# An expert stage without engine barriers: the overfill flag loaded ahead, routing constants first, softmax weights behind the selection

## The reference

```python
def moe_swiglu(h, w_router, w_gu_e, w_dn_e):
    logits = (h @ w_router).astype(jnp.float32)          # 256 x 8
    top_val, top_idx = lax.top_k(logits, TOP_K)          # 2 of 8
    top_w = jax.nn.softmax(top_val, axis=-1)
    combine = jnp.sum(jax.nn.one_hot(top_idx, N_EXPERTS) * top_w[..., None], axis=-2)
    out = jnp.zeros_like(h)
    for e in range(N_EXPERTS):
        out = out + combine[..., e:e + 1] * swiglu(h, w_gu_e[e], w_dn_e[e])
    return out
```

## Time and profile before

| | us |
|---|---|
| median of 3 runs | 2953.33 |
| lowest, highest | 2951.13, 2954.88 |
| profiled execution, its own time | 2958.39 |
| its span in the trace | 2956.6 |
| PE busy, share of the span | 2781.0, 94% |
| DVE, ACT, POOL busy | 1777.8, 1478.7, 39.9 |
| granted PE clock, mean | 0.975 |

### The profile page before, as it was taken

How to read it: one execution, slowest core, us unless ns; L and a number is a source line. 1 busy time by engine, 2 the same in 40 slices (tenths; PEclk the granted TensorE clock), 3 DMA queues, 4 the chain that set the end, 5 groups by cost and what they waited for, 6 DMA issues and landing times.

```text
span 2956.6 us, 40705 instructions
## 1 busy us (share of the span) xinstructions
PE 2781.0 (94%) x14700; PEld 2199.6 (74%) x14700; DVE 1777.8 (60%) x2624; ACT 1478.7 (50%) x2344; POOL 39.9 (1%) x50
## 2 busy tenths in 40 slices
PE   7999999998799999899999999899999799989998
PEld 6667777766688888777776667677777577667887
DVE  4656665655688888544455544664564446455776
ACT  5535565553567767433334343553453434444654
POOL 0000000000000000000000100000000010000000
PEclk9999999999899999999999999999999899999999
DMA  6436885443699999321231212354453234333564
GB/s 210 129 101 185 258 250 184 128 136 107 217 320 310 333 314 308 122 80 51 79 89 51 75 58 79 102 163 127 136 171 100 59 99 121 93 97 104 146 183 143
DMA packets 352396, 444.82 MB, mean 150 GB/s; under 512 B 19569, under 2 KB 197873, under 8 KB 352225
## 3 DMA queue, kind: packets, MB, share of 16 engines
q1 hardware_dynamic: 349792, 435.44, 46.9%
q0 software_dynamic: 2144, 6.74, 0.7%
q10 hardware_dynamic: 288, 0.36, 0.0%
HBM read 441.43 MB, written 1.05 MB: 150 GB/s over the span
## 4 chain that ended last, share of the span: by engine, by line
PE 48%; ACT 4%; DVE 4%; issue 3%; PEldq 0%; ACTq 0%; DVEq 0%
PE ps L2219 12%; PE ps L2260 10%; PE ps L2232 6%; PE ps L2273 5%; PE ps L2264 3%; PE ps L2573 1%; PE ps L2207 1%; PE ps L2280 1%; PE ps L2556 1%; ACT w_hi L987 1%; PE ps L2463 1%; PE ps L2593 1%; PE ps L2418 1%; DVE att L1967 1%; PE ps L2562 1%
## 5 line engine op out<-in xcount | busy, mean ns | idle before, releaser
L1463 DVE TENSOR_TENSOR w_lo<-raw,w_hi 128x1024 fp32r<-128x1024 f32 (+1 forms) x674 | 800.2, 1200 | 577.0 <-ACT w_hi L987 488.8
L987 ACT ACTIVATE w_hi<-raw 128x1024 fp32r<-128x1024 f32 (+1 forms) x674 | 687.5, 1034 | 346.6 <-PE ps L2232 151.9
L2260 PE MATMUL ps<-w_hi,h_hi 128*128 128x512 f32 (+1 forms) x992 | 406.9, 412 | 21.6 <-DVE h_lo L1881 14.0
L2260 PE MATMUL ps<-w_hi,h_lo 128*128 128x512 f32 (+1 forms) x992 | 383.3, 389 | 0.0
L2219 PE MATMUL ps<-h_hi,w_hi 128*128 128x256 f32 (+1 forms) x1008 | 299.2, 322 | 7.5 <-DVE arena L1491 3.7
L2273 PE MATMUL ps<-w_lo,h_hi 128*128 128x512 f32 (+1 forms) x992 | 300.6, 387 | 0.0
L2219 PE MATMUL ps<-h_lo,w_hi 128*128 128x256 f32 (+1 forms) x1008 | 296.5, 319 | 0.0
L2260 PEld LDWEIGHTS ps<-w_hi,h_hi 128*128 128x128 f32 x992 | 189.9, 191 | 62.2 <-DVE h_lo L1881 16.3
L2219 PEld LDWEIGHTS ps<-h_hi,w_hi 128*128 128x128 f32 x1008 | 192.1, 191 | 35.3 <-ACT w_hi L987 11.2
L2232 PE MATMUL ps<-w_hi,act_hi 128*128 128x512 f32 x528 | 216.1, 409 | 0.5 <-ACT w_hi L987 0.5
L2273 PEld LDWEIGHTS ps<-w_lo,h_hi 128*128 128x128 f32 x992 | 184.9, 190 | 40.5
(11 more groups left out here) (286 smaller groups left out, 4329.1 us busy)
## 6 DMA issues: line engine op xcount, KB each, us to landing
raw<-in_w_in SPq DMA_DIRECT2D x196, 512.0 KB, 3.6
raw<-in_w_mod SPq DMA_DIRECT2D x96, 512.0 KB, 4.6
raw<-in_w_up SPq DMA_DIRECT2D x88, 512.0 KB, 4.0
raw<-in_w_gu_exp SPq DMA_DIRECT2D x64, 512.0 KB, 5.3
arena<-in_w_gu_exp SPq DMA_DIRECT2D x64, 512.0 KB, 5.0
arena<-in_w_gu_exp SPq DMA_DIRECT2D x64, 384.0 KB, 3.9
arena<-in_w_dn_exp SPq DMA_DIRECT2D x48, 512.0 KB, 6.3
raw<-in_w_gu_dense SPq DMA_DIRECT2D x44, 512.0 KB, 5.0
```

The costliest lines, as they stand in the source:

```text
L987: nc.scalar.activation(w_hi[:, half, 0:n], place[:, 0:n], ACT.Copy).then_inc(seg.sig.hi_ready, 1)
L1463: nc.vector.tensor_tensor(w_lo[:, half, 0:n], place[:, 0:n], w_hi[:, half, 0:n].bitcast(F32), ALU.subtract).then_inc(seg.sig.lo_ready, 1)
L2260: ins = mm(ps[:, 2 * h + p % 2, 0:width], x[:, k + c, p * P:(p + 1) * P], wh[:, c * width:(c + 1) * width], start=opens and c == 0 and x i ...
```

## The change

No engine barrier is left. The flag is loaded into a register on ACT, DVE and PE in the experts' first tokens and kept to the end of the loop; if the second copy of the segment is entered, three engines meet before and after it (inside the branch). SP is as before. The router's segment no longer splits the experts' first two units at its end; ACT and DVE do so in `first_tokens`. ACT makes `XN` after the logits are copied, and takes an exponential of a constant behind it. In `route` DVE makes the constants before it waits for the logits, then only the masks and places; the softmax weights (`weigh`) come after `select` and the two splits. Halves of the first tokens are made one after the other, and PE waits for the second half only at the unit that reads it (in every expert). `gather` waits for `XN`, `route` for the logits, the next norm for `accumulate`.

```diff
+                router.routes = True
+                half, used, _ = router.uses[0][0]
+                add("route", logits=logits, route=route, buf=buf, ready=(half_saved[half], used + 1), src=plan[-2])
+                router_step = plan[-1]
                 took(pe=2, d=3, a=1)
-                meet()
...
+                        seg.clear, seg.routed = mixed, router_step
...
-                    meet()
...
+                done = (experts_main.accumulated, M + 2 * N_EXP)
+                turn_norm([0], gain, shift, Y_AT + 1024, by=["dve", "act"], ready=[done] * TT, turned_ctx=ctx_turned)
...
@@ ACT @@
             def first_tokens(seg):
+                if seg.routed is not None:
+                    st = seg.routed
+                    for j in range(AHEAD):
+                        split(seg, 0, j)
+                    act.wait_ge(stage_dve, st.at["d"] + 1)
+                    nc.scalar.activation(st.route[:, :, 49:50], st.route[:, :, 48:49], ACT.Exp).then_inc(stage_act, 1)
+                    act.wait_ge(stage_dve, st.at["d"] + 3)
+                    fullest_now.append(act.value_load(seg.buf["flag"], min_val=0, max_val=T))
                 for half in range(2):
                     upper_half(seg, 0, half)
...
-                    if seg.next:
+                    if seg.next and not seg.routes:
                         split(seg.next, 0, j)
...
+            def route(st):
+
+                act.wait_ge(inverse_done, st.src.at["norm"] + 1)
+                for t in st.src.tiles:
+                    ins = nc.scalar.activation(XN[:, t, :], x_tm[:, t, :], ACT.Copy, scale=rms[:, X_ROOT + t:X_ROOT + t + 1])
+                ins.then_inc(tokens_ready, 1)
+                nc.scalar.activation(rms[:, 29:30], eps[:, :], ACT.Exp)
...
-                    most = act.value_load(st.seg.flag, min_val=0, max_val=T)
-                    with act.If(most > P):
+                    with act.If(fullest_now[0] > P):
+
+                        act.drain().then_inc(at_overflow, 1)
+                        act.wait_ge(at_overflow, 3)
                         stream(st.seg)
+                        act.drain().then_inc(at_overflow, 1)
+                        act.wait_ge(at_overflow, 6)
...
@@ DVE @@
             def first_tokens(seg):
                 select(seg, 0)
+                if seg.routed is not None:
+                    for j in range(AHEAD):
+                        split(seg, 0, j)
+                    weigh(seg.routed)
+                    fullest_now.append(dve.value_load(seg.buf["flag"], min_val=0, max_val=T))
                 for half in range(2):
                     gain(seg, 0, half)
-                for half in range(2):
                     lower_half(seg, 0, half)
...
             def route(st):
                 r = st.route
+
+                nc.vector.tensor_scalar(st.buf["upto"], anti[:, 0, 0:P].bitcast(F32), 0.0, None, ALU.is_equal)
+                settled(nc.vector.memset(st.buf["sel"], 1.0))
+                settled(nc.vector.tensor_tensor_scan(st.buf["slot_no"], st.buf["sel"].rearrange("p t n -> p (t n)"),
+                                                     st.buf["sel"].rearrange("p t n -> p (t n)"), 0.0, ALU.mult, ALU.add))
+                settled(nc.vector.memset(r[:, :, PLACE:PLACE + 32], 0.0))
                 dve.wait_ge(stage_pe, st.at["pe"] + 1)
...
+                dve.wait_ge(stage_dve, st.at["d"] + 1)
+                for t in range(TT):
+                    for c in range(2):
+                        ins = nc.vector.tensor_scalar(r[:, t, 16 + 8 * c:24 + 8 * c], expert_no[:, :], r[:, t, 40 + c:41 + c], None,
+                                                      ALU.is_equal)
+                settled(ins)
+                nc.vector.tensor_tensor(r[:, :, TAKES:TAKES + 8], r[:, :, 16:24], r[:, :, 24:32], ALU.add).then_inc(stage_dve, 1)
+                dve.wait_ge(stage_pe, st.at["pe"] + 2)
...
@@ PE @@
-                if seg.mode == "moe" and q == 0 and opens:
-                    pe.wait_ge(seg.ex.xg_done, 2 * it + (M + 2))
+                if seg.mode == "moe" and q == 0 and k in (0, DC // 2):
+                    pe.wait_ge(seg.ex.xg_done, 2 * it + (M + 1 + 2 * k // DC))
...
             def gather(seg, e, half):
 
+                pe.wait_ge(tokens_ready, 1)
...
+                if seg.routed is not None:
+                    pe.wait_ge(stage_dve, seg.routed.at["d"] + 3)
+                    fullest_now.append(pe.value_load(seg.buf["flag"], min_val=0, max_val=T))
                 body(0, True)
...
                 elif st.kind == "route":
+                    pe.wait_ge(*st.ready)
```

More of the change, by code:

```diff
@@ L375, in build @@
         halves = {}
-        count = {"barrier": 0, "sum": 0, "root": 0, "gate": 0, "tap": 0, "act": 0, "value": 0,
+        count = {"sum": 0, "root": 0, "gate": 0, "tap": 0, "act": 0, "value": 0,
                  "pe": 0, "a": 0, "d": 0, "max": 0, "bounded": 0, "bias": 0, "mod": 2, "norm": 0, "branch": 0, "x_ready": 0, "squared": 0, "summed": 0, "value_ready": 0, "diag": 0,
@@ L937, in _ @@
             for st in plan:
[L938 to L941, removed]
+                if st.kind == "bias":
                     nbias, l, last, free = st.bias
@@ L1433, in _ @@
                 elif st.kind == "route":
-                    act.wait_ge(stage_dve, st.at["d"] + 1)
-                    nc.scalar.activation(st.route[:, :, 49:50], st.route[:, :, 48:49], ACT.Exp).then_inc(stage_act, 1)
+                    route(st)
         @block.vector
@@ L2041, in route, with weigh @@
                 nc.vector.tensor_tensor(r[:, :, 48:49], r[:, :, 25:26], r[:, :, 24:25], ALU.subtract).then_inc(stage_dve, 1)
+                dve.wait_ge(stage_dve, st.at["d"] + 1)
[6 more added lines that the diff above has]
+                dve.wait_ge(stage_pe, st.at["pe"] + 2)
+                nc.vector.tensor_copy(r[:, :, PLACE:PLACE + 8], ps[:, 1, 0:TT * N_EXP].rearrange("p (t e) -> p t e", e=N_EXP))
+                settled(nc.vector.tensor_reduce(r[0:1, 0, 52:53], ps[0:1, 2, 0:N_EXP], AX.X, ALU.max))
+                nc.vector.tensor_copy(st.buf["flag"], r[0:1, 0, 52:53]).then_inc(stage_dve, 1)
+                dve.wait_ge(stage_dve, st.at["d"] + 3)
+            def weigh(st):
+                r = st.route
                 dve.wait_ge(stage_act, st.at["a"] + 1)
@@ L2157, in _ @@
                 elif st.kind == "overflow":
-                    most = dve.value_load(st.seg.flag, min_val=0, max_val=T)
-                    with dve.If(most > P):
+                    with dve.If(fullest_now[0] > P):
+                        dve.drain().then_inc(at_overflow, 1)
+                        dve.wait_ge(at_overflow, 3)
                         stream(st.seg)
-                elif st.kind == "barrier":
-                    dve.drain().then_inc(at_barrier, 1)
-                    dve.wait_ge(at_barrier, 4 * (st.at["barrier"] + 1))
+                        dve.drain().then_inc(at_overflow, 1)
+                        dve.wait_ge(at_overflow, 6)
                 elif st.kind == "turn":
@@ L2616, in _ @@
                 elif st.kind == "overflow":
-                    most = pe.value_load(st.seg.flag, min_val=0, max_val=T)
-                    with pe.If(most > P):
+                    with pe.If(fullest_now[0] > P):
+                        pe.drain().then_inc(at_overflow, 1)
+                        pe.wait_ge(at_overflow, 3)
                         stream(st.seg)
-                elif st.kind == "barrier":
-                    pe.drain().then_inc(at_barrier, 1)
-                    pe.wait_ge(at_barrier, 4 * (st.at["barrier"] + 1))
+                        pe.drain().then_inc(at_overflow, 1)
+                        pe.wait_ge(at_overflow, 6)
                 elif st.kind == "route":
+                    pe.wait_ge(*st.ready)
                     for t in range(TT):
```

43 lines of the change are left out of this document (11 added, 32 removed).

## The result

The changed kernel takes 2942.24 us (median of 6 runs, 2933.0 to 2946.72) where the kernel before, run beside it, takes 2953.68 (2951.13 to 2954.88): a ratio of 0.9962, 95% interval 0.9951 to 0.9974, so 11.4 us less. A second pair of series on another chip gave 0.997 (0.9959 to 0.9981; 11 runs after, median 2943.45); one run of before there, of 9471 us, stands outside that ratio, as does one of 3919 us of the last combined kernel outside its own. The forecast was 2939.7 with a range of 2936.0 to 2945.5.

The account below looks back on a forecast made before the run. PE was taken to bound the experts, with time to win only where PE stands still before and behind them. Gains 9.6 + 4.3 less 0.3 for added waits made 13.6: 2953.33 - 13.6 = 2939.7 us, range 2936 to 2945.5.

Parts of the forecast that it names:

- What bounds it: Experts are bound by PE, busy 55.0 of 55 us, so bringing their first product forward moves all that follows.
- added waits: In the expert loop, 24 extra waits on PE cost 0.3 us, at most 1.9.
- weight stream: Rival (0.06): the experts' end hangs on the weights, not PE, so A is lost and B remains; 2949.3 us.
- loop that loses its place: Rival (0.04): shifted code no longer fits, so each of seven expert-loop turns costs a fetch; 2968 us, slower.
- Logits and routing: Router to gather: the logits' copy on DVE starts 4.0 us earlier, PE's gather 8.6 earlier (760.1, not 768.68).
- First tokens: After routing: DVE's chain, flag load last, ends at 764.9, PE's half gather at 763.9; first product 767.1 to 767.3.
- A: Gain 9.6 us (7.5 to 10.3), router's last product to first expert product; also that stretch's length.
- The jump: Behind the experts: without barriers DVE's 3.1 us jump overlaps `accumulate`, so its next work comes 3.4 us earlier.
- B: Gain 4.3 us (1.5 to 4.8), last scatter to the next tokens' products; also that stretch's length.
- the jump turns cheap: Rival (0.05): code behind the experts' jump is already held, `accumulate` limits DVE; B = 5.2 + 0.9, 2937.9 us.
- The clock: Behind the experts: shorter PE pauses avoid the low clock, gaining 0.9 us, with 0 as the other end.
- only part comes: Rival (0.12): first-token steps grow, A = 7.0; DVE's jump waits for its fetch, B = 2.0; 2944.6 us.

Follow-up runs that it names:

- last combined kernel: Changed kernel with three edits: flags loaded at unit 29 of expert 0, square-sum behind the first split, ten idle products; 2932.7 us, ratio 0.9937.
- meeting put back: Changed kernel with the two barriers behind the experts and the flag load between them restored; 2943.06 us.
- sums one unit later: Changed kernel with DVE's square-sum behind the first split of `w_in_2` instead of ahead of it; B 13.02 us.
- splits back: Changed kernel with the splits of the experts' first two units back at the router's end, ahead of the logits' copy; A 16.13, B 14.54 us.
- no overflow copy: Changed kernel without the second copy of the experts' segment, so no flag loads or jumps; A 13.38, B 12.83 us.
- before once more: The kernel before, unchanged, profiled a second time; 2946.42 us.
- flag at unit 20: Changed kernel with the flag loaded on ACT, DVE and PE at unit 20 of expert 0; A 13.33, experts 434.26, B 15.59 us.
- weights at unit 20 too: Changed kernel with the flag load and DVE's softmax weights both at unit 20 of expert 0; A 13.58, experts 436.61, B 15.52 us.
- ten idle products: Changed kernel with ten unread 128x512 products on PE behind the last scatter; B 12.94 us.

## Why the prediction was right, and where it was not

**What bounds it.** Right. The experts took 433.82 us against 433.81, and PE was busy 55.00 of 55 us in the stretch that answers the second of the earlier trace rows. The added waits, put at 0.3, cost 0.0; the rivals of the weight stream and of the loop that loses its place are dead, as either would have shown in this number.

**Logits and routing.** Right step by step: the copy stands 0.32 us behind the start of the last product (predicted 0.28 + 0.05), DVE's copy of the turned logits 1.18 (1.3), the gather 7.35 where 760.1 - 752.57 = 7.5 was predicted.

**First tokens.** Predicted A was 9.6, measured 9.92. The chain was the predicted one, with DVE's flag load last: `weigh` ended 11.1 behind the router's last product (predicted 764.0 - 752.57 = 11.4), `gain` stood at 12.2 (12.3), and two experiments that took the load from this place gained 1.0 each. Not in the sum, though it decides what can be won further, is how near PE comes behind DVE: once DVE is 1 us earlier, taking more from DVE leaves `gain` waiting for the gather (1.62 us), and with the splits first it waits too (2.29). The low end of A's range had the gather take 7.6 us if the clock stayed low; where it did, it took 6.49.

**The jump.** Right: 3.4 us earlier were predicted for DVE, 3.6 came. The reading that carried it was that a list runs ahead of its engine: the branch stood on DVE's list at 1196.1, 0.02 behind `accumulate`'s start, and the next work began 3.0 later. The list shows 63 ns for that branch on DVE and 3737 for PE's, so the cost on DVE is seen only as the gap behind it; without the branch the first work behind `accumulate` stands 1.5 us earlier. The Trainium skill, page "Runtime: NRT & Kernel Launch", section "Instruction fetch mechanics", had a taken far branch wait for a fetch; the trace agrees, with these 3.7 us and the instruction packets beside them. The Trainium skill, page "Advanced Engine Details and Errata", section "Control Flow Timing", had about 108 ns; this jump took 35 times as long. The prediction gave B 2.7 more by that figure; by its own end of `accumulate`, ahead of which DVE can't go on, it would have been 1.8 (6.1 - 4.3, as in the rival "the jump turns cheap"), and the kernel without any jump gained 1.5 in waiting.

**The clock.** Wrong, and in sign. I took 0.9 us as gained because both new pauses (3.2 and 2.0) were shorter than the time for which PE had stood at full clock before. The pauses were 2.2 and 2.5, and the 44 products took longer. Before is at 1.2 GHz from within the first of these two rows of its PE until within the second:

```profile
1216.00:1218.00 2.00, 0.00 (x0) 0.72 0.05 12
...
1222.00:1224.00 2.00, 2.00 (x11) 0.57 0.21 20
```

That is from 1216.9 to 1223.7, 6.8 us, of which 4.8 fell into the pause and 2.0 on products. After was low from 1199.9 to 1206.8, 6.8 us too, but its products began at 1201.5 and stood in it for 5.2. The same rows in us-wide steps give for other kernels (first the time at the low level around this pause, then how much of it lay behind the start of the 44 products, then their length in the chain of waits):

| kernel | low, us | of it on the 44 | the 44 |
| --- | --- | --- | --- |
| before | 6.8 | 2.0 | 6.39 |
| meeting put back | 6.8 | 2.3 | 6.56 |
| sums one unit later | 3.4 | 3.0 | 6.83 |
| splits back | 6.8 | 3.3 | 6.96 |
| no overflow copy | 3.4 | 3.4 | 7.03 |
| before once more | 10.2 | 3.9 | 7.24 |
| after, both profiles | 6.8 | 5.2 | 7.83 |
| flag at unit 20 | 6.8 | 5.8 | 8.09 |
| weights at unit 20 too | 6.8 | 5.6 | 8.00 |
| ten idle products, and all three edits | 0 | 0 | 5.53 |

Each us of low clock on the products costs 0.44 us over the 5.53 without any, and with these two numbers all the lengths come out within 0.03. Counted from the last scatter's start the low stretch lay from 6.2 to 13.1 in before and from 5.9 to 12.7 in after: starting the products 3.6 us sooner did not shorten it, but moved work into it. Starting them another 1.1 us sooner, with the sums one unit later, did: there it lay from 5.9 to 9.3. By the two profiles of before the change lost (5.2 - 2.0) x 0.44 = 1.4 or (5.2 - 3.9) x 0.44 = 0.6 us, where I had 0.9 gained. So B was 2.2 to 3.0 and not 4.3: the one term of the sum that was off by more than 0.4.

**The sum.** 9.9 + 2.2 = 12.1 (12.9 with the second profile of before) instead of 13.6, and 11.4 between the medians (7.8 on the other chip, where before ran at 2951.24). By the number alone the rival "only part comes" (2944.6) is as near to the measured 2942.24 as the forecast (2939.7) is. The stretches tell them apart: the rival had A at 7.0, where 9.9 came, and its B of 2.0 lies near the measured 2.2, but for a jump that would hold DVE longer, and the jump came as forecast. That the total came so near the forecast is in part luck: A, the jump and the added waits each came 0.2 to 0.3 better than predicted and hid a part of the clock's 2.3. The rival "the jump turns cheap" has nothing for it: the fetch is still 3.7 us on PE's list.

## What to carry to other kernels

A barrier hides what each engine's list could do ahead: look for the list's own place (a drain or a branch that starts long before its engine is free) to see how much of a jump or a load will lie beside other work once the barrier is gone. When a pause is shortened, look in the trace where the low clock then falls, not only whether the pause is shorter; if products will stand in it, a few idle ones behind the last real one are worth their place. And after a move ask which engine is next to be late, and don't take room on an engine from its average: at 48 of 55 us busy, DVE had a unit with no room at all.

## What the runs showed of the hardware

- The low clock around this pause lasted 3.4, 6.8 or 10.2 us and nothing between, and it was absent with idle products in the pause; the kernel before had 6.8 in one profile and 10.2 in the other. I had expected one length for one program, and that it would end sooner by as much as PE worked sooner.
- A register load of one word of on-chip memory took 550 ns on the list and 1.0 us on the path; with the meeting put back the later load of the same word took 0.28 to 0.33 us.
- Identical code differs by steps of about 1.7 us, and each step is one more piece of low clock. One stretch between the same two products, far behind the change, shows it (bounds, length, busy us, granted clock, DMA share, GB/s; before, then before once more, then after):

```profile
1267.10:1308.10 41.00, 40.12 (x166) 0.92 0.26 78
1260.90:1300.20 39.30, 38.42 (x165) 0.96 0.28 81
1248.30:1290.90 42.60, 41.72 (x165) 0.88 0.26 75
```

  Summed in shorter rows the low clock is 6.8, 3.4 and 10.2 us of the stretch. With 3.4 it took 39.3 to 39.4 us in six kernels (before once more, no overflow copy, the later sums, the idle products, the splits back, all three edits), with 6.8 it took 40.9 to 41.0 in four (before, the meeting put back, the flag and the weights at unit 20), and with 10.2 it took 42.6 in both profiles of after.
- The whole stretch behind B follows too: 1721.1 to 1730.4 us over the twelve profiles, with 71 us at the low clock for the shortest and 88 for the longest. The mean clock goes with the total: of after's first six runs the fastest (2933.0) had 0.982, the slowest (2946.7) 0.976. So a single pair of spans, as the 17.0 us above, can be off by 5 us, and only stretches cut at the same instructions can be compared.
- Both profiles of after have the most low clock behind B, those of before less (84 and 71 us), and the seven single edits made on after less as well (71 to 84). Whether the change itself gives something back there is open; no run told it from the scatter.
